# Weight fetches of a two-column merge, of a key block and of a kernel's start, each released by another condition

## The reference

```
gates = sigmoid(gate_logits + b_gate)            # 2 branches x 1024
merged = gates[0] * (o_a @ w_proj_a) + gates[1] * (o_b @ w_proj_b)
x = x + merged @ w_out
x = x + moe_ffn(rmsnorm(x))                      # top 4 of 32 experts
```

```
merged = sum over n of sigmoid(g_logits[n] + gate_b[n]) * (y[n] @ w_branch[n])   # 3 branches
x = x + rmsnorm(merged @ w_out)
```

## Time and profile before

| | before |
|---|---|
| median of 3 runs | 3232.08 us (3229.14 to 3233.04) |
| profiled execution | 3231.61 us, span 3229.8 us |
| PE busy | 2969.3 us, 92% of the span |
| DVE / ACT / POOL busy | 1222.8 / 758.8 / 117.6 us |
| DMA | 577.58 MB, mean 179 GB/s |
| mean granted clock of PE | 0.962 |

### The profile page before, as it was taken

The page is one execution under the profiler, slowest core; times in us unless marked ns, Lnnn a source line. Parts: engine busy times, 40 slices in busy tenths (PEclk is TensorE's granted clock), DMA queues, the critical chain, the costliest instruction groups (busy, mean ns, idle before and its releaser), DMA issues.

```text
span 3229.8 us, 43238 instructions
## 1 busy us (share of the span) xinstructions
PE 2969.3 (92%) x15332; PEld 2064.4 (64%) x15333; DVE 1222.8 (38%) x2554; ACT 758.8 (23%) x1499; POOL 117.6 (4%) x132
## 2 busy tenths in 40 slices
PE   7989888986999989899899969898989899989898
PEld 6874666653586547376356758586766596767674
DVE  5770773223211222222221155535333355443332
ACT  2221651111211121211211113514111225232111
POOL 0000000000000000000000000011000000110000
PEclk9999999976999999999999979999999999999999
DMA  4212012244999999999999453022212230112221
GB/s 167 79 66 78 2 40 77 67 195 186 356 400 332 418 419 400 402 393 385 396 419 394 162 197 106 1 85 67 91 64 67 75 116 27 59 59 98 66 79 65
DMA packets 137659, 577.58 MB, mean 179 GB/s; under 512 B 15965, under 2 KB 21341, under 8 KB 87360
## 3 DMA queue, kind: packets, MB, share of 16 engines
q1 hardware_dynamic: 128032, 558.87, 45.4%
q0 software_dynamic: 9504, 17.07, 1.4%
HBM read 572.47 MB, written 20.97 MB: 184 GB/s over the span
## 4 chain that ended last, share of the span: by engine, by line
PE 82%; DVE 7%; DMA 6%; ACT 2%; issue 2%; DVEq 1%; SPq 0%; ACTq 0%; POOLq 0%
PE banks L389 30%; PE banks L1496 13%; PE banks L1472 9%; PE banks L1001 7%; PE banks L326 7%; PE banks L1446 6%; DMA arena<-in_w_experts 5%; PE banks L774 2%; PE banks L797 2%; PE banks L785 2%; DVE arena L847 1%; PE banks L271 1%; DMA arena<-in_w_in 1%; DVE arena L859 1%; PE banks L1425 1%
## 5 line engine op out<-in xcount | busy, mean ns | idle before, releaser
L389 PE MATMUL banks<-arena 128*128 128x256 f32 (+2 forms) x4704 | 1022.1, 378 | 49.3 <-DVE arena L1066 30.5
L389 PEld LDWEIGHTS banks<-arena 128*128 128x128 f32 x4704 | 887.8, 192 | 173.3 <-issue 50.8
L1496 PEld LDWEIGHTS banks<-arena 128*128 128x128 f32 x3584 | 404.0, 193 | 14.4 <-issue 14.4
L1496 PE MATMUL banks<-arena 128*128 128x128 f32 x3584 | 405.8, 276 | 4.6 <-issue 4.6
L1472 PE MATMUL banks<-arena 128*64 128x512 f32 (+1 forms) x1024 | 322.5, 593 | 0.0
L1446 PE MATMUL banks<-arena 128*64 128x512 f32 x1152 | 270.4, 620 | 19.7 <-DMA arena<-in_w_experts 16.9
L1574 DVE TENSOR_TENSOR arena<-banks,arena 128x512 f32<-128x512 f32 x64 | 44.2, 691 | 613.9 <-PE banks L1496 351.9
L424 ACT ACTIVATE arena<-banks 128x512 f32<-128x512 f32 (+2 forms) x168 | 98.8, 588 | 723.9 <-PE banks L389 723.9
L326 PE MATMUL banks<-arena 128*128 128x512 f32 x576 | 249.9, 593 | 1.0 <-DMA arena<-in_w_in 1.0
L440 DVE TENSOR_TENSOR arena<-banks,arena 128x512 f32<-128x512 f32 (+2 forms) x126 | 85.6, 680 | 429.8 <-PE banks L389 428.0
L1472 PEld LDWEIGHTS banks<-arena 128*64 128x64 f32 (+1 forms) x1024 | 123.5, 159 | 176.1 <-issue 176.0
(11 more groups left out here) (209 smaller groups left out, 2073.1 us busy)
## 6 DMA issues: line engine op xcount, KB each, us to landing
arena<-in_w_experts SPq DMA_DIRECT2D x384, 1024.0 KB, 19.3
arena<-in_w_in SPq DMA_DIRECT2D x84, 1024.0 KB, 5.0
arena<-in_w_out SPq DMA_DIRECT2D x12, 1024.0 KB, 5.1
arena<-in_w_branch SPq DMA_DIRECT2D x24, 512.0 KB, 4.8
arena<-expert_rows SPq DMA_DIRECT2D x4, 2048.0 KB, 14.5
arena<-in_w_in SPq DMA_DIRECT2D x4, 832.0 KB, 4.5
arena<-in_gate_b SPq DMA_DIRECT2D x2, 1536.0 KB, 6.6
arena<-in_x SPq DMA_DIRECT2D x4, 512.0 KB, 5.2
```

Of the source, the lines that this page charges most:

```text
L389: last = PE.matmul(PS[:, bank, t * width:(t + 1) * width], one[:, t * P:(t + 1) * P], other, start=(first and t == 0 and kk == 0), stop=(t ...
L1496: last = PE.matmul(PS[:, q, f * P:(f + 1) * P], gate_up(q, k)[:, f * P:(f + 1) * P], xT[:, k], start=(f == 0 and k == 0), stop=(f == 3 and ...
```

## The change

- `dense_sp` no longer uses the drains after DVE's results 0 and 1. `w0_free` now counts only plain products (a new count `D` beside them). The upper half waits for it and for the third difference and product 0 of the block before, the lower for its fourth difference and product 4. The semaphore `w1_free` and the two drains are gone.
- In a merge stage the lower half waits for the `mm` count of the stage's start (`done=-n * nbr`) instead of the half's.
- `begin` is run ahead of the wait for the upper weights.
- The identity is a transfer of its own with its own semaphore; the other constants are fetched behind the first weights. PE's first wait is for the identity. DVE still waits for constants and gains.
- The key block goes to its own buffer at SC + 2048. DVE no longer waits for the query transposes there; PE turns query tiles 0 and 1 ahead of products 5 and 6 and tiles 2 and 3 inside the first V block; ACT copies partials 0 to 2 first, and tiles 2 and 3 of the queries after the key block; DVE makes all four differences of the key block ahead of query tiles 2 and 3.

```diff
-        def dense_sp(sp, c, k, src, plain=0, quartered=0):
-            L = c.of("L") + k
+        def dense_sp(sp, c, k, src, plain=0, quartered=0, done=None):
+            D_, F = c.of("D") + plain, c.of("F") + quartered
+            M = c.of("M") + (plain if done is None else done)
             for h in range(2):
                 dst, s_ = src(h)
                 if h == 0:
-                    sp.wait_ge(SEM["w0_free"], up(L))
+                    sp.wait_ge(SEM["w0_free"], up(D_))
+                    sp.wait_ge(SEM["mixed_w"], up(4 * F - 1))
+                    sp.wait_ge(SEM["part_mm"], up(7 * F - 6))
                 else:
-                    sp.wait_ge(SEM["mm"], up(4 * (c.of("M") + plain)))
-                    sp.wait_ge(SEM["w1_free"], up(c.of("F") + quartered))
+                    sp.wait_ge(SEM["mm"], up(4 * M))
+                    sp.wait_ge(SEM["mixed_w"], up(4 * F))
+                    sp.wait_ge(SEM["part_mm"], up(7 * F - 2))
                 sp.dma_start(dst, s_).then_inc(SEM["w0_in" if h == 0 else "w1_in"], 16)
...
+                if "begin" in hooks:
+                    hooks["begin"]()
                 pe.wait_ge(SEM["w0_in"], 16 * L + 16)
...
                 V.tensor_tensor(to, one, self.part((0, 2, 3, 3)[i], w), ALU.add).then_inc(SEM["ev"], 1)
-                if i < 2:
-                    V.drain().then_inc(SEM["w1_free" if i else "w0_free"], 1)
...
-                return {(0, 0): begin, (0, 1): lambda: pe.wait_ge(SEM["tr_free"], up(c.of("tr") + 4)),
+                return {"begin": begin, (0, 1): lambda: pe.wait_ge(SEM["tr_free"], up(c.of("tr") + 4)),
...
-                pe.wait_ge(SEM["const_in"], 16)
+                pe.wait_ge(SEM["ident_in"], 16)
...
+            staged = v2(*cfg.get("staged", (SC, TT, 512)))
+            late = "staged" in cfg
...
-                if prev:
+                if late:
+                    hooks = {(5, 0): turn(0), (6, 0): turn(1)}
+                elif prev:
                     hooks = {(2, 0): turn(0), (2, 1): turn(1), (5, 0): turn(2), (6, 0): turn(3)}
...
                 Q1.act(act, c, k, k, 0, n)
+                if late:
+                    Q1.act(act, c, k, k, 1, n)
+                    Q1.act(act, c, k, k, 2, n)
+                    back(0)
+                    Q1.act(act, c, k, k, 3, n)
+                    back(1)
+                    for tt in range(TT):
+                        square(tt)
+                        root(tt)
+                    return
...
-                        if prev:
+                        if prev and not late:
                             qk_wait(dve, c, tt + 1)
...
                         if tt and next_n:
-                            Q1.mix(dve, c, k + 1, next_n, (0, 1))
+                            Q1.mix(dve, c, k + 1, next_n, (0, 1, 2, 3) if next_n < 512 else (0, 1))
...
-                if next_n:
+                if next_n == 512:
                     Q1.mix(dve, c, k + 1, next_n, (2, 3))
...
-                 "ins": lambda tt: [ST[tt][:, 0:P]],
+                 "ins": lambda tt: [v(SC + 2048 + 256 * tt, P)], "staged": (SC + 2048, TT, 256),
...
-                sp.dma_start(v(CON, NCONST), A["consts"]).then_inc(SEM["const_in"], 16)
+                sp.dma_start(v(CON, P), A["consts"][:, 0:P]).then_inc(SEM["ident_in"], 16)
                 heads_1.lead(sp, c)
+                sp.dma_start(v(CON + P, NCONST - P), A["consts"][:, P:NCONST]).then_inc(SEM["const_in"], 16)
...
+                        def turn_queries(tt):
+                            if tt in (0, 2):
+                                eng.wait_ge(SEM["qk_ready"], up(c.of("qk_ready") + 24 + tt // 2 + 3))
+                                tr_pe(eng, c, 26 + tt // 2, cfgQB["ins"](2 + tt // 2))
...
-                                     None if i else turn_keys)
+                                     None if i else turn_keys, early=None if i else turn_queries)
                     if who == "act":
+                        for tt in (2, 3):
+                            tr_out(eng, "act", c, 24 + tt, cfgQB["dst"](c, 6, tt), 4)
...
-                            dense_sp(sp, c, b, gate_weights(c0, n, b), quartered=b)
+                            dense_sp(sp, c, b, gate_weights(c0, n, b), quartered=b, done=-n * nbr)
```

More of the change, by code:

```diff
@@ L165, in build @@
         Wh = [v2(W, 4, 512), v2(W + 2048, 4, 512)]
-        names = ("x0_in x1_in x2_in x3_in x_nat x_done post_in gains_in const_in mask_in grow_in norm_sq norm_ms norm_sd norm_h tr tr_free "
-                 "w0_in w1_in w0_free w1_free wb0_in wb1_in mm ev qk_sq qk_ms qk_sd qk_ready "
+        names = ("ident_in x0_in x1_in x2_in x3_in x_nat x_done post_in gains_in const_in mask_in grow_in norm_sq norm_ms norm_sd norm_h tr tr_free "
+                 "w0_in w1_in w0_free wb0_in wb1_in mm ev qk_sq qk_ms qk_sd qk_ready "
                  "biased qk sm p_rdy normed pt_rdy pt_free pv o_done "
@@ L183, in build @@
         BASE = 16
-        FROM_ZERO = set("mla_in x0_in x1_in x2_in x3_in x_nat post_in gains_in const_in mask_in grow_in w0_in w1_in wb0_in wb1_in h2_out gb_in gathered slot_in ch0 ch1 ch2 "
+        FROM_ZERO = set("ident_in mla_in x0_in x1_in x2_in x3_in x_nat post_in gains_in const_in mask_in grow_in w0_in w1_in wb0_in wb1_in h2_out gb_in gathered slot_in ch0 ch1 ch2 "
                         "ch3 ch4 ch5 ch6 ch7 ch8 ch9 ch10 ch11 scattered bdown_in comb0 comb1 comb2 comb3 x_out ws_in bias_rows0 "
@@ L591, in square @@
                     if cfg.get("v_out"):
-                        AC.activation(cfg["v_out"](tt), ST[tt][:, nh * E:n], ACT.Copy)
+                        AC.activation(cfg["v_out"](tt), staged[:, tt, nh * E:n], ACT.Copy)
                     act.wait_ge(SEM["qk_ms"], up(c.of("qk_ms") + 4 * k + tt - 1 if k + tt else c.of("qk_ms")))
-                    AC.activation(SQ[tt][:, 0:nh * E], ST[tt][:, 0:nh * E], ACT.Square).then_inc(SEM["qk_sq"], 1)
+                    AC.activation(SQ[tt][:, 0:nh * E], staged[:, tt, 0:nh * E], ACT.Square).then_inc(SEM["qk_sq"], 1)
                 def root(tt):
@@ L615, in dve_ @@
             def dve_(dve, c):
-                to = v2(SC, TT, 512)
                 for tt in range(TT):
                     ms = v(SM + 16 + 8 * tt, nh)
-                    st = ST[tt][:, 0:nh * E].rearrange("p (h e) -> p h e", h=nh)
+                    st = staged[:, tt, 0:nh * E].rearrange("p (h e) -> p h e", h=nh)
                     if tt % 2 == 0:
-                        if prev:
+                        if prev and not late:
                             qk_wait(dve, c, tt + 1)
-                        Q1.dve(dve, c, k, k, tt, to, n)
-                        Q1.dve(dve, c, k, k, tt + 1, to, n)
+                        Q1.dve(dve, c, k, k, tt, staged, n)
+                        Q1.dve(dve, c, k, k, tt + 1, staged, n)
                         if tt and next_n:
-                            Q1.mix(dve, c, k + 1, next_n, (0, 1))
+                            Q1.mix(dve, c, k + 1, next_n, (0, 1, 2, 3) if next_n < 512 else (0, 1))
                     dve.wait_ge(SEM["qk_sq"], up(c.of("qk_sq") + 4 * k + tt + 1))
@@ L740, in project_first @@
             counts["T"] = counts["L"] = 11
-            counts["M"] = 3
+            counts["M"] = counts["D"] = 3
             return Stage(counts, sp=sp_, pe=qk_program("pe"), act=qk_program("act"), dve=qk_program("dve"), lead=lead, fenced=False)
@@ L1148, in pe_ @@
                     norm_ffn.turn(pe, c, tt)
-            return Stage({"T": 2, "L": 2, "M": 2, **NORM}, sp=sp_, pe=pe_, dve=dve_, act=act_, lead=lead, fenced=False)
+            return Stage({"T": 2, "L": 2, "M": 2, "D": 2, **NORM}, sp=sp_, pe=pe_, dve=dve_, act=act_, lead=lead, fenced=False)
         R = SC
@@ L2092, in dve_ @@
                     norm_pre.scale(dve, c, TT - 1)
-            return Stage({"T": 2, "L": 2, "M": 2, "post_ms": 4, "post_sd": 4, **NORM}, sp=sp_, pe=pe_, act=act_, dve=dve_, lead=lead, fenced=False)
+            return Stage({"T": 2, "L": 2, "M": 2, "D": 2, "post_ms": 4, "post_sd": 4, **NORM}, sp=sp_, pe=pe_, act=act_, dve=dve_, lead=lead, fenced=False)
         load = constants()
```

## The result

| | before | after |
|---|---|---|
| median, same chip | 3232.56 us (3229.14 to 3238.49) | 3195.53 us (3192.14 to 3196.45) |
| ratio | | 0.9882, 95% interval 0.9864 to 0.9899 |
| profiled execution | 3231.61 us, span 3229.8 us | 3195.03 us, span 3193.2 us |
| PE busy | 2969.3 us | 2969.0 us |
| mean granted clock of PE | 0.962 | 0.965 |

The account below looks back on a forecast made before the run. PE was taken to bound the kernel (82% of the chain), so only its idle or slow time counts. Merges -37.3, start -4.0 and key block +1.6 sum to -39.7 us: 3192 us forecast, range 3187 to 3200.

Parts of the forecast that it names:

- The merges: Three turns between column halves: 30.5 us of PE idle time and 6.8 us of slow matmuls go, 37.3 us together.
- 5 us of room: Merge turns: the lower half lands at about 525.6, DVE's second difference first reads it at 530.9.
- only the idle time: Merges return only the idle 30.5 us, as DVE comes late or PE still slows down: 3199 us, chance 0.12.
- the slower rival: Without gaps PE's granted clock falls to 1.2 GHz in the merges; one block in each gives 3265 us, chance 0.02.
- The start: Kernel start: PE begins at 13.5 instead of 17.6, the work chained to the transposes moves along; 4.0 us gained.
- The key block: First layer's key block, up to the V products: a net loss of 1.6 us, ends -1.0 and +3.1 us.
- later root: Key block: DVE's extra differences delay query tile 2's reduction, then root, ACT's copy and PE's fourth product, +1.7 us.
- query transposes in V: Two groups of query transposes leave the key block's gap and go into the V products, +0.9 us of PE.
- weight wait: Before the V products: PE's wait for the V weights goes, as their upper half is free earlier, -1.0 us.
- The loss of 1.7 us in the slow records behind the gap: Key block: the 32 records after the gap took 5.63 us against 3.9 at full speed; this loss was assumed unchanged.
- The bound that a longer gap might add 1.5 us: Key block: slow records behind the longer gap could cost up to 1.5 us more, by the merges' largest loss.
- The conditions elsewhere and `begin` in later layers: New fetch conditions in steady gate and projection blocks, and earlier transposes in the two later layers: zero.

Follow-up runs that it names:

- the late fetch: Changed kernel, but at each merge turn the lower half is fetched only after the last branch product's first tile: 3212.53 us against 3238.59, ratio 0.9921.
- `apply` first: Kernel before, with DVE's four apply steps put ahead of the four weight differences at each merge turn: 3204.92 us against 3237.15, ratio 0.9907.

## Why the prediction was right, and where it was not

**The merges: right, in both terms.** Forecast 30.5 of idle time and 6.8 of slow records, 37.3 us; the three stages gave 12.2 + 13.2 + 11.9 = 37.3. The "5 us of room" is 4.8, by an estimate: by SP's timeline of merge 1 the two halves' issues ran from 502.23 to 516.43, the lower half's last, and with the 5.1 us of such a transfer it lands at about 521.5, against the second difference at 526.32.

```profile
502.23 14.20 SPq L303 DMA_DIRECT2D arena<-in_w_in  x2
```

That a gap ends 5.0 us after the landing, DVE's order being what it is, the late fetch and `apply` first showed from both sides. The rival "only the idle time" (3199) falls: the slow records went in all three. So does the slower rival: the 32 records took 6.91 us in all three, their length at full speed.

**The start: right, slightly large.** First transposes 13.62 (forecast 13.5), third product 26.96 (27), by the profile 4.0 us; DVE's row sums began at 25.63 (25.5), 2.6 us behind its second difference (2.3). Over all profiles it is 3.7, since the execution that I read had a late third product, 30.95 in a spread of 29.42 to 31.24. The working treated the weights as arriving 3 us before they are needed; with `begin` in its old place they would have been the limit, by 1.3 to 1.5 us.

**The key block: sign and two of three terms right, the sum too high.** Forecast +1.7 (later root), +0.9 (query transposes in V), -1.0 (weight wait), in all +1.6; the first pair of profiles has +0.5. The gap came out at 7.33 us (forecast 7.7), released by ACT as before. A single pair doesn't size terms of this kind, so here are all profiles. From block 6's last records to the fourth product they have 30.3 us in the four with the new staging and ACT's old order, and 28.6 in the three with the new conditions and the old staging: +1.7, as forecast. From there to the long V products they have 35.0 to 36.5 us, 35.5 on average, against 34.6: +0.9, as forecast. The step that was mis-sized is the third, the -1.0: the new conditions return 1.7 us (64.95 us on average in the five kernels with the old conditions, 63.2 with the new). 1.3 of these lie behind the fourth product, where PE's wait for the weights had been 0.9 to 1.7 us and not always the 0.98 that I read; 0.4 lie ahead of it, where I had put the effect of the drains at zero. So the key block costs +0.9 us on average, 0.7 less than forecast, and the +0.5 of the first pair has some luck in it.

The loss of 1.7 us in the slow records behind the gap, which I kept, varies: the 32 records took 5.20, 5.44, 5.33 and 6.73 us behind gaps of 7.33 or 7.34 us, 1.3, 1.5, 1.4 and 2.8 over full speed, 1.8 on average. The largest, from the kernel with the late fetch:

```profile
216.95 6.73 PE L395 MATMUL banks<-arena 128*128 128x128 f32 x32 [7.34 <-ACT arena L432]
```

The bound that a longer gap might add 1.5 us was thus not idle: one of four added 1.1. The Trainium skill (TensorE: Matmul & The Clock Gate, "What's actually happening") says that the clock follows how busy the array has been recently; I had drawn from it that a longer gap lengthens the slow stretch. The rows do not bear that out as a rule: 7.3 us of gap cost 1.3 to 2.8, 4.8 to 5.2 cost 1.7 to 2.0 and, at the turns, 5 us cost 3.0 on average where 10 cost 2.3.

**The conditions elsewhere and `begin` in later layers: put at zero.** `begin` is zero: the stage behind the experts took 47.4 us after and 49.2 before, but 47.6 also in the two kernels with the old `begin` and the merge edit. The conditions elsewhere gave 0.4 us in blocks 0 to 6, where the drains had been put at zero.

**What the sum left out** is the rest of the kernel. The steps themselves came to -41.1 instead of -39.7; untouched stages took 4.5 back, above all latent attention, +8.4 us at a granted clock of 0.89 and 0.87 where it was 0.98 and 0.93 (in the second profiles of both kernels +4.5). I had asked what the clock does beside the gaps only. That a forecast which left this out missed by only 3.5 us is partly luck: the surplus of the steps hid 1.4 of the 4.5. For the second layer the 4.7 us go with merge edit and new conditions together, as forecast for that run, with the late fetch as the one exception; by what path a stage in which no instruction is changed and which begins hundreds of us behind the nearest turn gets another clock stays open. For the first layer the same code gave both lengths. The router's 2.8 us are of this kind too: its 64 records took 11.0 to 11.9 us in six of the eight profiles with both edits, and 13.9 in all others.

## What to carry to other kernels

Look for a wait that was right in one part of a loop and is inherited in another: here a counter of finished products guarded a buffer whose own readers had long been through. To price it, follow what stands in program order behind the instruction that waits for the data, up to the release of the bank that PE needs: the landing has to come ahead of PE's end by that work (5 us here), not just ahead of it. And where an engine's in-order program puts a copy that PE waits for behind a chain of another engine (ACT's root behind DVE's norm), moving work into or out of that gap is worth a microsecond or two; moving the copy was worth 3.3 us here, and 7.3 with DVE's sums moved along with it.

## What was not expected of the hardware

- A 5 us gap of PE cost as much in slow records as one of 10 us: 3.3, 3.1 and 2.7 us in its one profile, against 1.6 to 3.1 at the twelve turns of the four kernels with a 10 us gap. Halving the gap left 7.9 of the 12.4 us of a turn.
- The same records of a partly busy stage ran at a granted clock between 0.87 and 0.98: 71.7 to 78.1 us in the first layer, 73.1 to 78.1 in the second.
- SP issued the first weights at 3.87 us before and at 6.22 after. The kernel with the new conditions alone has the same 6.22, that with the new start alone 3.64, so it comes from the new conditions; that they wait for semaphores whose first values POOL sets is argued, not tried. It costs nothing by itself: with the conditions alone the weights landed at 6.22 + 10.47 = 16.7, in the kernel before at 17.2. The transfers ahead of them kept the queue busy: from 4 to 17 us of before it moved 381 to 393 GB/s. The SP rows after:

```profile
3.19 0.57 SPq L701 DMA_DIRECT2D arena<-in_consts  x1
6.22 0.94 SPq L303 DMA_DIRECT2D arena<-in_w_in  x2
7.21 0.53 SPq L703 DMA_DIRECT2D arena<-in_consts  x1
```
